# Inverting the recurrence's chunk triangles in 32 x 32 blocks on four places of the array instead of 64 x 64

## What is computed

```python
def _rwkv7_scan(s0, r, w, k, v, a, b):
    # for each token, for each head, with the state S (64 x 64):
    #   S = S * w + (S a) b^T + v k^T;   y = S r
    s_fin, ys = lax.scan(step, s0, xs)
```

## Time and profile before

| | |
|---|---|
| median of three | 3650.43 us (3649.68 to 3650.66) |
| profiled execution | 3646.23 us, span 3644.4 us |
| TensorE products / weight loads busy | 3410.7 us (94%) / 3006.3 us (82%) |
| VectorE / ScalarE busy | 2498.6 us (69%) / 1878.8 us (52%) |
| data moved | 723.31 MB, mean 198 GB/s |
| before the recurrence (0 to 372 us) | clock 0.87, 149 GB/s |
| recurrence, context (372 to 516) and latent (581 to 723) | see the rows below |
| between the two (516 to 581) | clock 0.71, 212 GB/s, `rwprep` and late modulation weights |
| the rest (723 to 3644) | 2921 us, TensorE busy 2816.6 us, clock 0.98, 222 GB/s |

### The profile page before, as it was taken

How to read it: one execution, slowest core, us unless ns; L and a number is a source line. 1 busy time by engine, 2 the same in 40 slices (tenths; PEclk the granted TensorE clock), 3 DMA queues, 4 the chain that set the end, 5 groups by cost and what they waited for, 6 DMA issues and landing times.

```text
span 3644.4 us, 70946 instructions
## 1 busy us (share of the span) xinstructions
PE 3410.7 (94%) x27148; PEld 3006.3 (82%) x27148; DVE 2498.6 (69%) x3329; ACT 1878.8 (52%) x2496; POOL 6.3 (0%) x17
## 2 busy tenths in 40 slices
PE   5987887889999898999999999999999999999998
PEld 3864866879899767788888888887998899998898
DVE  3677566555555456899999999998557555558555
ACT  3333131234444444788878888887435634445633
POOL 0000000000000000000000000000000000000000
PEclk8987998999999998999999999999999999999999
DMA  5224113025455412899999999997554355554354
GB/s 200 93 98 190 50 49 112 20 87 184 156 173 183 152 53 74 288 362 363 360 361 360 361 363 363 362 364 269 171 183 133 111 184 173 172 181 136 106 184 156
DMA packets 199351, 723.31 MB, mean 198 GB/s; under 512 B 21888, under 2 KB 25472, under 8 KB 198784
## 3 DMA queue, kind: packets, MB, share of 16 engines
q1 hardware_dynamic: 198576, 714.01, 55.2%
q0 software_dynamic: 592, 6.69, 0.5%
HBM read 719.57 MB, written 1.05 MB: 198 GB/s over the span
## 4 chain that ended last, share of the span: by engine, by line
PE 83%; DVE 10%; ACT 3%; DMA 2%; issue 1%; SPq 1%; DVEq 0%; ACTq 0%
PE ps L306 24%; PE ps L307 23%; PE ps L308 23%; PE ps L1523 1%; PE ps L530 1%; DMA ada_late<-wada 1%; PE ps L1520 1%; PE ps L662 1%; PE ps L1514 1%; PE ps L2195 1%; PE ps L2144 1%; DVE w_lo L269 1%; PE ps L2214 1%; DVE tt L1611 1%; DVE rs L540 1%
## 5 line engine op out<-in xcount | busy, mean ns | idle before, releaser
L269 DVE TENSOR_TENSOR w_lo<-w_raw,w_hi 128x1024 fp32r<-128x1024 f32 x529 | 647.1, 1225 | 724.8 <-ACT w_hi L265 721.3
L265 ACT ACTIVATE w_hi<-w_raw 128x1024 fp32r<-128x1024 f32 x529 | 558.4, 1058 | 791.4 <-PE ps L308 735.6
L306 PE MATMUL ps<-a_hi,w_hi 128*128 128x256 f32 (+1 forms) x3012 | 899.6, 299 | 54.7 <-DVE a_lo L557 24.5
L2280 DVE TENSOR_TENSOR mlo<-mraw,mhi 128x1024 fp32r<-128x1024 f32 x726 | 877.3, 1223 | 92.7 <-ACT mhi L2276 64.1
L307 PE MATMUL ps<-a_lo,w_hi 128*128 128x256 f32 (+1 forms) x3012 | 899.0, 298 | 0.0
L308 PE MATMUL ps<-a_hi,w_lo 128*128 128x256 f32 (+1 forms) x3012 | 897.0, 298 | 0.0
L2276 ACT ACTIVATE mhi<-mraw 128x1024 fp32r<-128x1024 f32 x726 | 770.5, 1062 | 183.3 <-PE ps L308 144.2
L306 PEld LDWEIGHTS ps<-a_hi,w_hi 128*128 128x128 f32 x3012 | 581.4, 193 | 79.5 <-issue 51.8
L307 PEld LDWEIGHTS ps<-a_lo,w_hi 128*128 128x128 f32 x3012 | 575.6, 191 | 15.4 <-issue 0.5
L308 PEld LDWEIGHTS ps<-a_hi,w_lo 128*128 128x128 f32 x3012 | 575.5, 191 | 15.2
L306 PE MATMUL ps<-mhi,x_hi 128*128 128x512 f32 x968 | 395.9, 409 | 1.9 <-DVE mlo L2280 1.9
(11 more groups left out here) (503 smaller groups left out, 4377.6 us busy)
## 6 DMA issues: line engine op xcount, KB each, us to landing
mraw<-wexp SPq DMA_DIRECT2D x726, 512.0 KB, 5.3
w_raw<-wstream SPq DMA_DIRECT2D x529, 512.0 KB, 3.4
ada_late<-wada SPq DMA_DIRECT2D x80, 512.0 KB, 6.1
ada_raw<-wada SPq DMA_DIRECT2D x16, 512.0 KB, 9.2
bia<-bias POOLq DMA_DIRECT2D x1, 4096.0 KB, 13.8
con<-consts SPq DMA_DIRECT2D x1, 1824.0 KB, 16.0
conb<-constsb POOLq DMA_DIRECT2D x1, 1224.0 KB, 8.2
hT<-ctxT SPq DMA_DIRECT2D x1, 1024.0 KB, 12.4
```

Source lines behind the costliest of these rows:

```text
L265: nc.scalar.activation(whi[:, slot, :], raw[:, slot, :], ACT.Copy).then_inc(hi_ready.sem, 1)
L269: nc.vector.tensor_tensor(wlo[:, slot, :], raw[:, slot, :], whi[:, slot, :].bitcast(F32), ALU.subtract).then_inc(lo_ready.sem, 1)
L306: nc.tensor.matmul(out, lhs[0], rhs[0], start=start, stop=False, skip_group_check=skip)
L2280: nc.vector.tensor_tensor(mlo[:, slot, :], mraw[:, rslot, :], mhi[:, slot, :].bitcast(F32), ALU.subtract).then_inc(lo_ready.sem, 1)
```

## The change

For T of 64 it inverts the two diagonal blocks of RB = 32 first, in four levels, and joins them in a last one.

- `quads(fn)` issues sixteen products for one d: pair m, head e, half j, on partitions 64e + 32j. Each is 32 x 32 with 32 columns, on the place (64e + 32j, 64e + 32j), so four different places stand side by side.
- L1500 is replaced by two `quads`: N's two diagonal blocks and their transposes, from K = 64 rows into 32 partitions of output each. They lie compactly, 2 x 4 x 32 columns of a bank.
- VectorE, for each d: one 128x256 mask of both into `tt`, one 128x256 addition of the identity (`i32`), one 128x512 operation that makes `nl` for all four levels at once from the same bank (mask `lvn`), then `br` with another mask (`mo`: its first half keeps only the off-diagonal block of N) and `kr` as before. Masks by level between the additions are gone.
- In the four levels x is 16 products for each d (before 8 of 64 x 64), t is 32 (before 16); ScalarE's copy has 128 columns (before 256) and VectorE's addition 256 (before 512).
- The last level: x = `br`'s off-diagonal block against the first block's T, K = 32, 64 output partitions, 32 columns, eight products for each d; ScalarE copies it into `xw`, whose other half stays zero (one memset, in the context segment's `rwprep`; it lies on the buffer of `rs`); t is eight products of the same form. Meanwhile VectorE spreads the two blocks into `tf` (64 x 64) by a mask `bd`, one 128x256 operation for each d, and then adds the joined part (128 columns, `tT_done`). U uses `tf`.
- The constants shrink from 4032 to 3168 columns.

```diff
-CONSTS = [("ident", 128), ("ones", 128), ("bones", 128), ("i64", 64),
-          ("mx", 256), ("lv", 2 * (RLEV + 1) * 2 * 64), ("scan64", 1024),
+CONSTS = [("ident", 128), ("ones", 128), ("bones", 128), ("i32", 32),
+          ("mx", 256), ("mo", 256), ("lv0", 128), ("lvn", 256), ("bd", 64), ("scan64", 1024),
...
+            ("xs", [P, 2, 4, RB]), ("nl", [P, 2, 4, 4, RB]), ("tf", [P, 2, 4, RC]), ("btt", [P, 2, 4, RC]),
+        xw = sb("xw", [P, 2, 4, RC], at=rs_at)
...
+                link(nc.vector.memset(xw[:], 0.0))
...
+        def quads(fn):
+            for m in range(4):
+                for e in range(2):
+                    for j in range(2):
+                        last = fn(m, e, slice(64 * e + RB * j, 64 * e + RB * (j + 1)), j)
+            return last
...
-                heads_of(d, lambda d, m, e: nc.tensor.matmul(
-                    ps[hp(e), 4 + d, col(m)], ar[hp(e), d, m, ch[d], 0, :], bt[hp(e), d, m, cs[d]],
+                rows = lambda j: slice(ch[d] * RC + RB * j, ch[d] * RC + RB * (j + 1))
+                quads(lambda m, e, q, j: nc.tensor.matmul(
+                    ps[q, 4 + d, qcol(m)], ar[hp(e), d, m, ch[d], 0, RB * j:RB * (j + 1)], bt[hp(e), d, m, rows(j)],
+                    start=True, stop=True))
+                quads(lambda m, e, q, j: nc.tensor.matmul(
+                    ps[q, 4 + d, qcol(m, 1)], bt[hp(e), d, m, rows(j)], ar[hp(e), d, m, ch[d], 0, RB * j:RB * (j + 1)],
                     start=True, stop=True)).then_inc(*S("n_ps").one)
...
-            for lv in range(RLEV):
+            for lv in range(RLEV - 1):
                 for d in range(2):
                     pe.wait_ge(*S("lv_in").next("pe"))
+                    quads(lambda m, e, q, j: nc.tensor.matmul(ps[q, d, qcol(m)], nl[q, d, lv, m, :], tt[q, d, 0, m, :],
+                                                              start=True, stop=True)).then_inc(*S("x_ps").one)
                 for d in range(2):
                     pe.wait_ge(*S("x_sb").next("pe"))
+                    quads(lambda m, e, q, j: nc.tensor.matmul(ps[q, 2 + d, qcol(m)], tt[q, d, 1, m, :], xs[q, d, m, :],
+                                                              start=True, stop=True))
+                    quads(lambda m, e, q, j: nc.tensor.matmul(ps[q, 2 + d, qcol(m, 1)], xs[q, d, m, :],
+                                                              tt[q, d, 1, m, :], start=True, stop=True)
+                          ).then_inc(*S("t_ps").one)
+            first = lambda d, e: slice(64 * e + RB * d, 64 * e + RB * (d + 1))
+            second = lambda d, e: slice(64 * e + RB * (1 - d), 64 * e + RB * (2 - d))
+            for d in range(2):
+                pe.wait_ge(*S("lv_in").next("pe"))
+                heads_of(d, lambda d, m, e: nc.tensor.matmul(
+                    ps[hp(e), d, qcol(m)], br[first(d, e), d, m, 0:RC], tt[first(d, e), d, 0, m, :],
+                    start=True, stop=True)).then_inc(*S("x_ps").one)
+            for d in range(2):
+                pe.wait_ge(*S("x_sb").next("pe"))
+                heads_of(d, lambda d, m, e: nc.tensor.matmul(
+                    ps[hp(e), 2 + d, qcol(m)], xw[second(d, e), d, m, :], tt[second(d, e), d, 1, m, :],
+                    start=True, stop=True)).then_inc(*S("t_ps").one)
...
-                    nc.scalar.activation(xs[:, d, :, :], bank(d), ACT.Copy).then_inc(*S("x_sb").one)
+                    dst = xs[:, d, :, :] if lv < RLEV - 1 else xw[:, d, :, RB * d:RB * (d + 1)]
+                    nc.scalar.activation(dst, qbank(d), ACT.Copy).then_inc(*S("x_sb").one)
...
+                n2 = ps[:, 4 + d, 0:8 * RB].rearrange("p (s m l) -> p s m l", s=2, m=4)
+                link(nc.vector.tensor_tensor(tt[:, d, :, :, :], n2, bc(lv0[:, d, :, :].unsqueeze(2), [P, 2, 4, RB]),
+                                             ALU.mult))
+                t2_ = tt[:, d, :, :, :].rearrange("p s m l -> p (s m) l")
+                link(nc.vector.tensor_tensor(t2_, t2_, bc(cc("i32").unsqueeze(1), [P, 8, RB]), ALU.add))
+                link(nc.vector.tensor_tensor(nl[:, d, :, :, :], bc(n2[:, 1, :, :].unsqueeze(1), [P, RLEV - 1, 4, RB]),
+                                             bc(lvn[:, d, :, :].unsqueeze(2), [P, RLEV - 1, 4, RB]), ALU.mult))
+                link(nc.vector.tensor_tensor(br[:, d, :, :], b4(d), bc(mo[:, d, :].unsqueeze(1), [P, 4, P]), ALU.mult))
                 link(nc.vector.tensor_tensor(kr[:, d, :, :], b4(2 + d), bc(mx[:, d, :].unsqueeze(1), [P, 4, P]),
                                              ALU.mult))
-                link(mask_n(0, d))
                 dve.sem_inc(S("lv_in").sem, 1)
+            for lv in range(RLEV - 1):
                 for d in range(2):
+                    t2_ = tt[:, d, :, :, :].rearrange("p s m l -> p (s m) l")
                     dve.wait_ge(*S("t_ps").next("dve"))
+                    link(nc.vector.tensor_tensor(t2_, t2_, qbank(2 + d, 8), ALU.add))
+                    dve.sem_inc(S("lv_in").sem, 1)
+            for d in range(2):
+                link(nc.vector.tensor_tensor(tf[:, d, :, :].rearrange("p m (j l) -> p m j l", j=2),
+                                             bc(tt[:, d, 1, :, :].unsqueeze(2), [P, 4, 2, RB]),
+                                             bc(bd.unsqueeze(1), [P, 4, 2, RB]), ALU.mult))
+            for d in range(2):
+                dve.wait_ge(*S("t_ps").next("dve"))
+                late = tf[:, d, :, RB * (1 - d):RB * (2 - d)]
+                nc.vector.tensor_tensor(late, late, qbank(2 + d), ALU.add).then_inc(*S("tT_done").one)
```

More of the change, by code:

```diff
@@ L39 @@
 RLEV = 5
+RB = 32
 MC = 128
@@ L131, in build @@
         sil = sb("sil", [P, 2, SEG])
+        rs_at = cursor[0]
         rs = sb("rs", [P, T2])
@@ L1229, in build @@
         ldd, cud, icd, eed = (ld0, ld1), (cu0, cu1), (ic0, ic1), (ee0, ee1)
-        br, kr, tt, xs, nl, btt, ktt, vtt, rh, uu, _r = lay(t0_, [
-            ("br", [P, 2, 4, P]), ("kr", [P, 2, 4, P]), ("tt", [P, 2, 2, 4, RC]),
-            ("xs", [P, 2, 4, RC]), ("nl", [P, 2, 2, 4, RC]), ("btt", [P, 2, 4, RC]),
+        br, kr, tt, xs, nl, tf, btt, ktt, vtt, rh, uu, _r = lay(t0_, [
+            ("br", [P, 2, 4, P]), ("kr", [P, 2, 4, P]), ("tt", [P, 2, 2, 4, RB]),
+            ("xs", [P, 2, 4, RB]), ("nl", [P, 2, 4, 4, RB]), ("tf", [P, 2, 4, RC]), ("btt", [P, 2, 4, RC]),
             ("ktt", [P, 2, 4, RC]), ("vtt", [P, 2, 4, RC]), ("rh", [P, 2, 4, RC]), ("uu", [P, 2, 4, RC])])
+        assert _r <= t0_ + 7 * 4 * 4 * SEG
+        xw = sb("xw", [P, 2, 4, RC], at=rs_at)
         assert _r <= ob
@@ L1481, in col, with qcol @@
             return slice((half * 4 + m) * RC, (half * 4 + m + 1) * RC)
+        def quads(fn):
[4 more added lines that the diff above has]
+            return last
+        def qcol(m, half=0):
+            return slice((half * 4 + m) * RB, (half * 4 + m + 1) * RB)
         def pe_solve(pe, seg, n):
@@ L1558, in bank, with qbank @@
             return ps[:, i, half * 256:half * 256 + n * RC].rearrange("p (m l) -> p m l", l=RC)
+        def qbank(i, n=4):
+            return ps[:, i, 0:n * RB].rearrange("p (m l) -> p m l", l=RB)
         def act_solve(act, n):
@@ L1578, in dve_solve @@
             ch = (n, NRC - 1 - n)
-            lvm = cc("lv").rearrange("p (s v d l) -> p s v d l", s=2, v=RLEV + 1, d=2)
             mx = cc("mx").rearrange("p (d l) -> p d l", d=2)
[L1581 to L1586, removed]
+            mo = cc("mo").rearrange("p (d l) -> p d l", d=2)
+            lv0 = cc("lv0").rearrange("p (d s l) -> p d s l", d=2, s=2)
+            lvn = cc("lvn").rearrange("p (d v l) -> p d v l", d=2, v=RLEV - 1)
+            bd = cc("bd").rearrange("p (j l) -> p j l", j=2)
             dve_bonus(dve, link, seg, n)
@@ L1590, in dve_solve @@
                 b4 = lambda i: ps[:, i, :].rearrange("p (m l) -> p m l", m=4)
[L1591 to L1597, removed]
@@ L1598, in dve_solve @@
-                link(nc.vector.tensor_tensor(tt[:, d, 1, :, :], tt[:, d, 1, :, :], e4, ALU.add))
+                n2 = ps[:, 4 + d, 0:8 * RB].rearrange("p (s m l) -> p s m l", s=2, m=4)
[3 more added lines that the diff above has]
+                link(nc.vector.tensor_tensor(t2_, t2_, bc(cc("i32").unsqueeze(1), [P, 8, RB]), ALU.add))
@@ L3030, in consts_a @@
     bones = np.kron(np.eye(2), np.ones((64, 64)))
-    i64 = np.tile(np.eye(RC), (2, 1))
+    i32 = np.tile(np.eye(RB), (4, 1))
     s, t = i[:, None], i[None, :]
@@ L3040, in consts_a @@
             lv[0, v, d], lv[1, v, d] = nn, nn.T
-    lv = lv.transpose(3, 0, 1, 2, 4).reshape(RC, -1)
+    mo = np.concatenate([lv[1, RLEV, 0], s <= t, lv[1, RLEV, 1], s >= t], 1)
+    block = lv[:, :, :, 0:RB, 0:RB]
+    lv0 = block[:, 0].transpose(2, 1, 0, 3).reshape(RB, -1)
+    lvn = block[1, 1:RLEV].transpose(2, 1, 0, 3).reshape(RB, -1)
+    bd = np.kron(np.eye(2), np.ones((RB, RB)))
     scan64 = np.tile((np.arange(1024) % RC != 0).astype(np.float32), (P, 1))
@@ L3046, in consts_a @@
     two = lambda a: np.tile(a, (2, 1))
```

(4 more changed lines are left out.)

5 lines of the change are left out of this document (1 added, 4 removed).

## The result

The changed kernel takes 3708.86 us (median; 3700.13 to 3715.04) against 3650.55 us of the kernel before beside it (3649.68 to 3651.71): ratio 1.0165, 95% interval 1.0151 to 1.018. It is 58 us slower where 52 us less was forecast, and the time lies outside the range. The profiled execution took 3713.45 us around a span of 3711.7 us.

What follows compares the result with a forecast made beforehand. The first block's recurrence was taken as bound by a chain of hand-overs between engines. Front 1.30 - 0.10, levels 5.2 and last level 0.14 gave 6.5 us a round, 52 for eight, less 0.5: 3599 us, range 3580 to 3645.

Steps and rivals of the forecast that it cites:

- What a record costs: TensorE products: four 32 x 32 places run side by side, four records per 33 ns, 8.3 ns each.
- the term of a level: Each of the four inverse levels: 2.10 us against 3.40, gaining 5.2 us a round.
- the place or the supply of instructions: TensorE's 64-column products: either can set the pace of a record per 29 ns, the densest sustained in the trace.
- Front, VectorE: VectorE ahead of the levels: five operations go, three come; 0.65 us less for each d, 1.30 us a round.
- Scores under the cover of the bonus: TensorE's scores ahead of the levels: 0.53 us against 0.47, hidden by VectorE's bonus operation except 0.1 us a round.
- ScalarE's copy as a new bound: In each level: the 128-element copy takes 0.28 us, so t of d = 1 starts at 0.83 us, not 0.80.
- Last level: From x of d = 1 to the right-hand sides: 1.71 us against 1.85, a gain of 0.14 us.
- It may no longer bring half clock, while each level now leaves TensorE idle: Granted clock, uncounted: shorter front wait may gain up to 9 us; levels idle TensorE some 0.5 us of 2.1.
- Rival C: TensorE: instruction supply sets 29.2 ns a record everywhere; level 5.43 us, 68 us lost, 3718 us; chance 0.12.
- Rival D: Levels: small places keep the granted clock at half; level 3.43 us, 50 us lost, 3701 us; chance 0.07.
- B: Levels: four places overlap only two by two, 16.6 ns a record; level 3.42 us, kernel 3641 us; chance 0.15.

Runs made afterwards that it cites:

- the first looped kernel: The changed kernel with each round's four 32 x 32 levels as a loop on TensorE: 3636.84 us, ratio 0.9963 to the kernel before.

## Why the prediction was wrong

It failed in one step, "What a record costs", and with it in the term of a level: 2.10 us in the sum, 5.45 us measured. The number there, 8.3 ns a record on four places, was nearly right for the array: 8.5 to 9.3 ns in the looped kernels at full clock. It came from a burst of eight records and was then used for 160 records of a level in a row, as though instructions were always at hand. At 8.3 ns a record TensorE uses an instruction every 4.2 ns; it gets one every 14 to 15. The step named that doubt ("the place or the supply of instructions"), and the choice between them was wrong. The burst could not speak on it: eight records are 16 instructions, and at the start of a round's levels 338 instructions ran off in 1.7 us before the first stop. What could have spoken was the queue's row for the stretch of 372 to 516 us of the kernel before, which the prediction did not read:

```profile
q8 instruction: 28, 0.46, 1.4%
```

28 packets of 256 are 7168 instructions, and TensorE has 2 x 3598 records there: the queue brings TensorE's code. A level had 192 instructions in 3.40 us, 17.7 ns each, already near the limit.

Point by point:

- Front, VectorE, 1.30 us less 0.10: 1.15 measured (9.40 to 8.25). Right; the block of d = 0 goes from br to br in 3.85 us before and in 3.21 now. Broadcasts with one more dimension cost nothing that shows: the operations before and after take 424 ns with 256 columns and 691 with 512.
- Scores under the cover of the bonus, 0.1 us a round for what comes through: behind the bonus operation of 467.90 VectorE waits 0.19 us for them, and 0.15 us of the 1.30 are missing in the front. Right within 0.1 us. No row separates the changes of place shape.
- A level, 2.10 us: 5.45. Wrong, by supply. Without that limit 2.61 to 2.65, of which the loop's own waits are 0.4 (0.32 ahead of x, 0.09 ahead of t). A level without both was not measured.
- ScalarE's copy as a new bound, 0.28 us for 128 elements: 277 ns. Right, and it is in the chain of the looped kernels.
- Last level, a gain of 0.14: from the end of the fourth addition to the first right-hand side 1.79 us before and 1.73 in the looped kernels, a gain of 0.06; in the changed one it is 2.87, mostly at half clock.
- "It may no longer bring half clock, while each level now leaves TensorE idle": the level's stops, which the sum did not have, brought it.
- Rival C had the mechanism and the size of a level: 5.43 (5.45). That its total came so near, 3718 us (3709), is in part luck. It priced every record at 29.2 ns, the scores too, which would have lost the front's gain, and four levels at the slow pace. But the front kept its gain, and the first level of a round did not grow (3.28 us for 3.55): as the stock of code at 434.97 shows, part of it had been fetched during the front's waits. And it had no half clock behind the levels, which cost 2.7 us a round. Its chance of 0.12 was too low: "no denser stretch exists" in 3644 us was the evidence, and it outweighed the burst.
- Rival D had the half clock right (0.71 to 0.73) and its cause wrong. B is excluded by the looped kernels.

The Trainium skill, Runtime: NRT & Kernel Launch, section "Instruction fetch mechanics", says that the fetch is in blocks of 16 KiB, 256 instructions, read ahead strictly in sequence, and that issue is slower than fetch, so it stays hidden. The block agrees with the packets above (0.02 MB each, 256 of 64 bytes). That it stays hidden does not: 43 stops over 0.9 us, 64 us, stand in the changed kernel's rounds, each behind a packet. The Trainium skill's floor of about 25 ns between starts (TensorE: Matmul & The Clock Gate, section "Wait — 56ns, not 53.3ns?"), which the prediction weighed, does not hold for the engine: 9 ns from record to record, in runs of 64; a single place starts one every 34 to 37 ns there, so as a floor of each place alone it is not contradicted.

Open: why it takes 1.2 to 1.6 us from a packet's landing to the next record, and what asks for a packet when (in the levels they mostly start 3.4 to 4 us apart). Also open is how to avoid the late first pass of the loops (2.49 us of "issue" at 422.50 in the first looped kernel); placing the loop's body against the packets was not tried, nor looping the whole round, nor plain waits inside the loop.

## What to carry to other kernels

Count the instructions of a straight stretch of TensorE, four for an fp32 product, and divide by its time: where that gives under 15 ns each for longer than what has been fetched ahead (some 340 instructions here), expect it to stop for its own code, as it did here, however small the products. A burst tells the array's pace and not the sustained one; look at the packets of the instruction queue and at "issue" in the waits. Smaller blocks save columns and cost instructions, so they want a loop. The loop's waits (0.4 us a level here) and its first pass, which is still fetched, belong into the sum.

## What the runs showed of the hardware beyond that

- Four 32 x 32 places do run side by side, sustained: 64 fp32 records start within 0.55 to 0.60 us at full clock.
- An instruction costs TensorE 14.2 to 15.7 ns in straight code (levels of 384 and 512 instructions: 5.45 and 7.46 us), under 5 ns from a loop, and 5 ns in straight code as long as the stock lasts (338 in 1.7 us).
- A loop's body of 384 instructions (24 KB) ran four times in each of eight rounds and was fetched once each time: 129 packets for 165.
- With stops of 1.3 to 2.0 us in each level, round 2 had the granted clock at half (1.2 GHz) from the second level on, and for 6.5 us behind the last stop in which TensorE was busy without a break (454.0 to 460.5); then it was full again.
- Filling a wait to hold the clock up worked (21 to 5 us at half) and was worth nothing measurable (1.0001, 0.9988 to 1.0014).
